# Layer 0 of a hybrid transformer kernel: another order of its first steps, and an end that works by halves of 512 columns

## The chip, the core and the metric

The kernel runs on one core of a Trainium2 chip, as one launch. The core has five engines with queues of their own: TensorE (PE, matrix products), VectorE (DVE), ScalarE (ACT), GpSimd (POOL) and SyncE (SP, which here only issues transfers). They meet at semaphores alone. The metric is the device time of the launch in microseconds.

## The reference

Two layers over 256 tokens of 1024 features, in float32. Each layer normalizes, projects to 13 groups of columns (`w_in`), runs four mixers on them (mLSTM, latent attention with rotary positions, gated linear attention, a convolution), normalizes by group and projects back (`w_out`). Layer 0 then has a dense SwiGLU, layer 1 a mixture of 8 experts of which each token uses two. A last normalization ends it.

```python
h = x
for l in range(DEPTH):                       # DEPTH = 2
    z = rms_norm(h, norm1_g[l]) @ w_in[l]
    (m_qk, m_v, m_o, m_if, a_cq, a_ckv, a_kr,
     g_q, g_k, g_v, g_r, g_a, c_glu) = split_cols(z, IN_SPLITS)
    y = jnp.concatenate([mlstm_mixer(...), mla_mixer(...), gla_mixer(...), conformer_conv(...)], axis=-1)
    h = h + group_rms_norm(y, fuse_g[l], N_GROUPS) @ w_out[l]
    u = rms_norm(h, norm2_g[l])
    f = swiglu(u, ...) if l % 2 == 0 else moe_ffn(u, ...)
    h = h + f
return rms_norm(h, final_norm_g)
```

## The kernel before, in words

Tokens lie on the 128 partitions in two tiles (t = 0, 1); `h[:, t, :]` holds 1024 features. Weights come in pieces of up to 2048 columns, 1 MB each, through a ring of 11 slots that SP fills; a slot is filled again when the piece in it has been split. A piece is split into `high` (ScalarE, line 725) and `low` (VectorE line 1141, for some pieces GpSimd line 622), in three buffers each. TensorE adds three products for each pair of factors (high times high, high times low, low times high); `piece_used` counts the pieces that it is done with and lets ScalarE split the piece three further on.

Every engine's order is written out by hand. In layer 0 the first pieces of `w_in` are `l0` (5 of the 8 blocks of features, 376 columns), `l1` (the other 3 blocks), `b`, `a`, `mq`, `mk` (256 columns, all 8 blocks). `half(name, 0)` and `half(name, 1)` are the two halves of a piece's products. For `l0` and `l1` the half is the token tile; tile 0 lands in bank 2 of PSUM and tile 1 in bank 1, and ScalarE copies them to `zl` (lines 869, 871). `b` lands in bank 0, `a` in bank 5.

Ahead of them TensorE transposes the normalized tokens, two blocks at a time (group g = 0 to 3 of tile t), into the banks of `START_BANKS[0][t][g]`; ScalarE and VectorE empty each bank to `uTh` and `uTl` (lines 759, 1158; `utl_ready` counts the emptied ones). `claim(b, sem, value)` makes TensorE wait until the former owner of bank b has let it go, and notes who lets it go next. Nine small products on bank 0 (line 1836) stand between the transposes and `l0`.

GpSimd first makes constants, issues 12 small loads and computes the angles of the rotary positions (`ang_ready`, line 606), then issues the loads of `walpha`, `uq` and `ukv`, then subtracts for `a`, `mq`, `mk`. ScalarE takes the sine of the angles between its splits of `b` and `a` (line 859, which needs another table of functions than `Ln` and `Exp`). The sines are used by GpSimd in the rotary step (line 662 on), once ScalarE has written the queries out (`q_out`).

At the end, the last expert's products of its hidden values with its last `down` piece fill banks 2 and 3. ScalarE writes both halves of the result as `yh`, VectorE the rest as `yl`; TensorE scatters them to the tokens (`scatter`, four banks); VectorE adds each half to `h` (`add_result`); ScalarE takes the squares of a whole tile, `Ln` and `Exp` for `rstd` (`norm`, `tile_rstd`); VectorE scales a whole tile and SP stores it.

## Time and profile before

| | |
|---|---|
| median of 3 runs | 1259.56 us (1256.64 to 1260.17) |
| the profiled execution's own time | 1260.54 us |
| its span in the trace | 1258.7 us |
| mean granted TensorE clock in it | 0.992 |
| TensorE busy | 98% of the span |
| VectorE, ScalarE, GpSimd busy | 77%, 67%, 14% |
| read from memory | 345.68 MB, 275 GB/s over the span |

The profile cuts the span in 40 slices of 31.5 us. TensorE's busy share is 9 tenths or more in all but the first and the last, which have 6. From about 440 us on, the eight experts follow each other, with memory at about 350 GB/s. Times in the trace are in microseconds from the start of the span; 1.84 us of the execution lie around the span.

### The profile page before, as it was taken

Reading aid. Unit: us, or ns where it says so; the run is one execution under the profiler, and the core shown is the slowest. Engines: PE = TensorE matmul, PEld = TensorE weight load, DVE = VectorE, ACT = ScalarE, POOL = GpSimd, SP = SyncE. Lnnn points to the kernel's source line nnn. Section 1 sums busy time; section 2 is a strip of 40 time slices with the busy share of each in tenths; the row PEclk is TensorE's granted clock in tenths of the full one; section 3 lists DMA queues with packets and bytes.
Section 4 is the critical chain, followed back from the end, with each engine's and each line's share of the span. In section 5 each row is a group of like instructions: output and inputs, shape, how many; then the busy total and the mean of one; then the engine's idle time right before and its main releaser. Section 6 shows DMA issues by size and latency. Waiting matters only on the chain.

```text
span 1258.7 us, 17374 instructions
## 1 busy us (share of the span) xinstructions
PE 1231.3 (98%) x6046; PEld 1026.4 (82%) x6046; DVE 963.1 (77%) x936; ACT 838.9 (67%) x883; POOL 177.4 (14%) x211
## 2 busy tenths in 40 slices
PE   6999999999999999999999999999999999999996
PEld 5888888888888878888888888888888888888885
DVE  4764654545485469999899889989989989988986
ACT  6667643344766767677776677777767767767774
POOL 8765100000486420000000000000000000000000
PEclk9999999999999999999999999999999999999998
DMA  9432975525243399999999999999999999999941
GB/s 305 142 136 67 348 253 181 187 83 168 77 152 125 104 346 353 353 347 364 358 340 361 358 346 353 356 357 352 357 350 349 353 349 358 352 356 347 370 176 52
DMA packets 168912, 347.40 MB, mean 276 GB/s; under 512 B 13166, under 2 KB 44032, under 8 KB 168864
## 3 DMA queue, kind: packets, MB, share of 16 engines
q1 hardware_dynamic: 167600, 344.43, 77.5%
q0 software_dynamic: 1232, 2.33, 0.8%
q8 instruction: 29, 0.48, 0.1%
q14 instruction: 19, 0.16, 0.0%
q10 hardware_dynamic: 32, 0.01, 0.0%
HBM read 345.68 MB, written 1.05 MB: 275 GB/s over the span
## 4 chain that ended last, share of the span: by engine, by line
PE 94%; DVE 3%; POOL 2%; ACT 1%; issue 1%; DVEq 0%; POOLq 0%; ACTq 0%
PE bank L1732 16%; PE bank L1734 16%; PE bank L1733 16%; PE bank L1752 8%; PE bank L1750 8%; PE bank L1751 8%; PE bank L1761 2%; PE bank L1697 2%; PE bank L1699 1%; PE bank L1698 1%; PE bank L1859 1%; PE bank L1860 1%; PE bank L1861 1%; DVE low L1141 1%; PE bank L2198 1%; PE bank L1924 1%
## 5 line engine op out<-in xcount | busy, mean ns | idle before, releaser
L1141 DVE TENSOR_TENSOR low<-ring,high 128x2048 fp32r<-128x2048 f32 (+1 forms) x302 | 684.4, 2286 | 108.9 <-ACT high L725 105.6
L725 ACT ACTIVATE high<-ring 128x2048 fp32r<-128x2048 f32 (+1 forms) x327 | 624.6, 1914 | 189.7 <-PE bank L1734 133.6
L1732 PE MATMUL bank<-high,uTh 128*128 128x512 f32 x880 | 349.7, 397 | 1.0 <-DVE low L1141 0.8
L1734 PE MATMUL bank<-high,uTl 128*128 128x512 f32 x880 | 343.7, 391 | 0.0
L1733 PE MATMUL bank<-low,uTh 128*128 128x512 f32 x880 | 343.5, 390 | 0.0
L1732 PEld LDWEIGHTS bank<-high,uTh 128*128 128x128 f32 x880 | 165.4, 188 | 40.3 <-DVE low L1141 6.3
L1734 PEld LDWEIGHTS bank<-high,uTl 128*128 128x128 f32 x880 | 165.3, 188 | 35.4
L1733 PEld LDWEIGHTS bank<-low,uTh 128*128 128x128 f32 x880 | 165.6, 188 | 32.2
L1750 PE MATMUL bank<-high,moe_hTh 128*128 128x512 f32 x352 | 137.9, 392 | 0.0
L1752 PE MATMUL bank<-high,moe_hTl 128*128 128x512 f32 x352 | 137.3, 390 | 0.0
L1751 PE MATMUL bank<-low,moe_hTh 128*128 128x512 f32 x352 | 137.1, 389 | 0.0
L622 POOL TENSOR_TENSOR low<-ring,high 128x512 fp32r<-128x512 f32 (+1 forms) x67 | 83.2, 1272 | 214.3 <-ACT high L725 210.3
L1752 PEld LDWEIGHTS bank<-high,moe_hTl 128*128 128x128 f32 x352 | 66.1, 188 | 13.8
L1751 PEld LDWEIGHTS bank<-low,moe_hTh 128*128 128x128 f32 x352 | 66.2, 188 | 13.4
L1750 PEld LDWEIGHTS bank<-high,moe_hTh 128*128 128x128 f32 x352 | 66.1, 188 | 13.4
L816 ACT ACTIVATE moe_hTh<-bank 128x512 fp32r<-128x512 f32 (+1 forms) x48 | 27.0, 563 | 66.6 <-PE bank L1761 66.6
L808 ACT ACTIVATE moe_sg<-bank 128x512 f32<-128x512 f32 (+1 forms) x48 | 27.0, 563 | 38.3 <-PE bank L1734 38.3
L1697 PE MATMUL bank<-uTh,high 128*128 128x256 f32 x160 | 48.5, 303 | 4.1 <-ACT zl L869 3.4
L1699 PE MATMUL bank<-uTh,low 128*128 128x256 f32 x160 | 47.5, 297 | 0.0
L1698 PE MATMUL bank<-uTl,high 128*128 128x256 f32 x160 | 47.4, 296 | 0.0
L1268 DVE SCALAR_TENSOR_TENSOR cacc<-bank,cols,cacc 128x255 f32<-128x255 f32 (+29 forms) x120 | 45.7, 458 | 0.1
L630 POOL TENSOR_TENSOR low<-ring,high 128x512 fp32r<-128x512 f32 x32 | 40.9, 1312 | 28.3 <-ACT high L725 28.0
(394 smaller groups left out, 1397.4 us busy)
## 6 DMA issues: line engine op xcount, KB each, us to landing
ring<-in_moe_w_up_dram SPq DMA_DIRECT2D x176, 512.0 KB, 5.5
ring<-in_moe_w_gate_dram SPq DMA_DIRECT2D x176, 512.0 KB, 5.4
ring<-in_moe_w_down_dram SPq DMA_DIRECT2D x176, 512.0 KB, 5.5
ring<-in_w_in_dram SPq DMA_DIRECT2D x36, 512.0 KB, 5.7
ring<-in_ffn_w_up_dram SPq DMA_DIRECT2D x22, 512.0 KB, 4.8
ring<-in_ffn_w_gate_dram SPq DMA_DIRECT2D x22, 512.0 KB, 4.6
ring<-in_ffn_w_down_dram SPq DMA_DIRECT2D x22, 512.0 KB, 4.6
ring<-in_w_out_dram SPq DMA_DIRECT2D x16, 512.0 KB, 4.0
```

Source lines behind the costliest of these rows:

```text
L622: last = pool.tensor_tensor(low[:, n % SPLIT, at], slot(n)[:, at], high[:, n % SPLIT, at].bitcast(F32), ALU.subtract)
L725: act.activation(high[:, n % SPLIT, 0:width], slot(n)[:, 0:width], ACT.Copy).then_inc(s["high_ready"], 1)
L1141: dve.tensor_tensor(low[:, n % SPLIT, 0:width], slot(n)[:, 0:width], high[:, n % SPLIT, 0:width].bitcast(F32), ALU.subtract).then_inc(s["l ...
L1697: pe.matmul(dst, ah, bh, start=first, stop=False)
L1698: pe.matmul(dst, ah, bl, start=False, stop=False)
L1699: last = pe.matmul(dst, al, bh, start=False, stop=final)
L1732: pe.matmul(o, ah, bh, start=(kd == 0), stop=False)
L1733: pe.matmul(o, ah, bl, start=False, stop=False)
L1734: last = pe.matmul(o, al, bh, start=False, stop=(kd == KD - 1))
L1750: pe.matmul(o, ah, bh, start=(c == 0 and f == 0), stop=False)
L1751: pe.matmul(o, ah, bl, start=False, stop=False)
L1752: last = pe.matmul(o, al, bh, start=False, stop=(c == LAST and f == 1))
```

## The change

It has two parts that share no code. **The start of layer 0.** Tile 0's transposes go to banks 2, 0, 1, 4 in place of 0, 4, 1, 2. TensorE takes both tiles of `l0` before `l1`. The nine small products wait for bank 0 but no longer make the `zl` copy its owner, so that `b` need not wait for it. ScalarE takes the sine later, behind the sigmoid of `b`, and the three mask copies ahead of the split of `a`. **The end.** The last `down` piece of each expert is multiplied half by half of its columns (`down_by_half`), and `yh`, `yl`, the scatter, the adds, the squares, the scaling and the stores go by halves of 512 columns, in the order of `LAST_ORDER`. One quarter of the output is scaled in another way: VectorE multiplies by the gain first, ScalarE by `rstd` after it, and ScalarE issues its store.

```diff
+        LAST_ORDER = ((0, 0), (1, 0), (0, 1), (1, 1))
-        START_BANKS = (((0, 4, 1, 2), (3, 5, 7, 6)), ((0, 1, 4, 7), (3, 4, 7, 0)))
+        START_BANKS = (((2, 0, 1, 4), (3, 5, 7, 6)), ((0, 1, 4, 7), (3, 4, 7, 0)))
+        scaled = moe_sg[:, 0, :]
...
-            for t in range(TT):
-                sp.wait_ge(s["out_ready"], t + 1)
-                sp.dma_start(out[0, t * P:(t + 1) * P, :], h[:, t, :]).then_inc(s["stored"], 16)
-            sp.wait_ge(s["stored"], 16 * TT)
+            sp.wait_ge(s["out_ready"], 2)
+            sp.dma_start(out[0, 0:P, :], h[:, 0, :]).then_inc(s["stored"], 16)
+            sp.wait_ge(s["out_ready"], 3)
+            sp.dma_start(out[0, P:2 * P, 512:D], h[:, 1, 512:D]).then_inc(s["stored"], 16)
...
                 split_in("b")
-                if l == 0:
+                if l:
+                    split_in("a")
+                else:
                     act.wait_ge(s["consts"], 1)
-                    act.wait_ge(s["ang_ready"], 1)
-                    act.activation(cossin[:, :, :, :], ang[:, :, :, :], ACT.Sin).then_inc(s["sin_ready"], 1)
-                    act.preload_act_table_set(LN_EXP)
-                split_in("a")
                 for out_, in_ in ((ident_r, ident), (mask_kr, mask_kt), (mask_qr, mask_qt)):
                     last = act.activation(out_[:, :], in_[:, :], ACT.Copy)
                 last.then_inc(s["masks_ready"], 1)
                 if l == 0:
-                    act.wait_ge(s["cols_ready"], 2)
+                    split_in("a")
...
                 act.activation(gsig[:, :, :], tiles2("b", 256), ACT.Sigmoid).then_inc(s["gsig_ready"], 1)
+                if l == 0:
+                    act.wait_ge(s["ang_ready"], 1)
+                    act.activation(cossin[:, :, :, :], ang[:, :, :, :], ACT.Sin).then_inc(s["sin_ready"], 1)
                 act.preload_act_table_set(LN_EXP)
...
             def result_high(n):
-                act.wait_ge(s["piece_used"], N_FFN * n + MOE0)
                 for i in range(2):
-                    last = act.activation(yh[:, i * 512:(i + 1) * 512], bank[2 + i][:, :], ACT.Copy, scale=wslot[:, :])
-                last.then_inc(s["yh_ready"], 1)
+                    if i == 0:
+                        act.wait_ge(s["acc_half"], n)
+                    else:
+                        act.wait_ge(s["piece_used"], N_FFN * n + MOE0)
+                    act.activation(yh[:, i * 512:(i + 1) * 512], bank[2 + i][:, :], ACT.Copy,
+                                   scale=wslot[:, :]).then_inc(s["yh_ready"], 1)
...
-            norm(3, u32[:, :, :].rearrange("p (t k) n -> p t (k n)", t=TT))
+            act.preload_act_table_set(LN_EXP)
+            squares = u32[:, :, :].rearrange("p (t k) n -> p t (k n)", t=TT)
+            for i, (t, half) in enumerate(LAST_ORDER):
+                act.wait_ge(s["h_ready"], 4 * 3 + i + 1)
+                at = slice(half * 512, (half + 1) * 512)
+                chain.done(act.activation(squares[:, t, at], h[:, t, at], ACT.Square, accum_out=ss[:, t, half:half + 1]))
+                chain.wait()
+                if half == 0:
+                    chain.done(act.activation(ss[:, t, 0:1], ss[:, t, 0:1], ACT.Copy, scale=1.0 / D, bias=EPS))
+                else:
+                    chain.done(act.activation(lnv[:, t, 0:1], ss[:, t, 1:2], ACT.Ln, bias=ss[:, t, 0:1], scale=1.0 / D))
+                    chain.wait()
+                    act.activation(rstd[:, t, 0:1], lnv[:, t, 0:1], ACT.Exp, scale=-0.5).then_inc(s["rstd_ready"], 1)
+            act.wait_ge(s["rstd_ready"], 10)
+            act.wait_ge(s["scaled_ready"], 1)
+            act.activation(h[:, 1, 0:512], scaled, ACT.Copy, scale=rstd[:, 1, 0:1]).then_inc(s["out_act"], 1)
+            act.wait_ge(s["out_act"], 1)
+            act.dma_start(out[0, P:2 * P, 0:512], h[:, 1, 0:512]).then_inc(s["stored"], 16)
...
-            for t in range(TT):
-                add_result(n_jobs, 2 * t)
-                add_result(n_jobs, 2 * t + 1)
-                dve.wait_ge(s["added"], 4 * n_jobs - (2 - 2 * t))
-                dve.memset(tiny[:, :], 0.0).then_inc(s["h_ready"], 2)
-            dve.wait_ge(s["rstd_ready"], 10)
+            for i, (t, half) in enumerate(LAST_ORDER):
+                dve.wait_ge(s["scat_ready"], 4 * n_jobs - (3 - i))
+                at = slice(half * 512, (half + 1) * 512)
+                dve.tensor_tensor(h[:, t, at], bank[SCATTER_BANKS[2 * t + half]][:, :], h[:, t, at],
+                                  ALU.add).then_inc(s["h_ready"], 1)
             dve.wait_ge(s["final_in"], 16)
-            for t in range(TT):
-                dve.scalar_tensor_tensor(out=h[:, t, :], in0=h[:, t, :], scalar=rstd[:, t, 0:1], in1=fin_g,
+            dve.wait_ge(s["h_ready"], 4 * 3 + 2)
+            dve.tensor_tensor(scaled, h[:, 1, 0:512], fin_g[:, 0:512], ALU.mult).then_inc(s["scaled_ready"], 1)
+            dve.wait_ge(s["h_ready"], 4 * 3 + 4)
+            for t, half in ((0, 0), (0, 1), (1, 1)):
+                at = slice(half * 512, (half + 1) * 512)
+                dve.wait_ge(s["rstd_ready"], 8 + t + 1)
+                dve.scalar_tensor_tensor(out=h[:, t, at], in0=h[:, t, at], scalar=rstd[:, t, 0:1], in1=fin_g[:, at],
                                          op0=ALU.mult, op1=ALU.mult).then_inc(s["out_ready"], 1)
...
+                def down_by_half(c):
+                    n = n0 + FFN_AT[("d0", c)]
+                    pe.wait_ge(s["hTl_ready"], at(c + 1))
+                    pe.wait_ge(s["low_ready"], pieces + (n + 1))
+                    for half in range(2):
+                        for f in range(2):
+                            bh, bl = part(n, f * 1024 + half * 512, f * 1024 + half * 512 + 512)
+                            pe.matmul(bank[accs[0][half]][:, :], hTh[:, f, 0, :], bh, start=False, stop=False)
+                            pe.matmul(bank[accs[0][half]][:, :], hTh[:, f, 0, :], bl, start=False, stop=False)
+                            last = pe.matmul(bank[accs[0][half]][:, :], hTl[:, f, 0, :], bh, start=False, stop=(f == 1))
+                        if half == 0:
+                            last.then_inc(s["acc_half"], 1)
+                    last.then_inc(s["piece_used"], 1)
...
-                    down(LAST, 0)
+                    down_by_half(LAST)
...
-                    claim(0, "zl_ready", 1)
+                    pe.wait_ge(*owner[0])
...
                 half("l0", 0, ("zl_ready", 2 * l + 1))
-                half("l1", 0)
                 if l:
+                    half("l1", 0)
                     start_transposes(l, 1)
                 half("l0", 1, ("zl_ready", 2 * l + 2))
+                if l == 0:
+                    half("l1", 0)
                 half("l1", 1)
...
-            scatter(n_jobs)
+            pe.wait_ge(s["selT_ready"], n_jobs)
+            for t, half in LAST_ORDER:
+                if t == 0:
+                    pe.wait_ge(s["yl_ready"], 2 * n_jobs - (1 - half))
+                o, at = bank[SCATTER_BANKS[2 * t + half]][:, :], slice(half * 512, (half + 1) * 512)
+                pe.matmul(o, selT[:, t, :], yh[:, at], start=True, stop=False)
+                pe.matmul(o, selT[:, t, :], yl[:, at], start=False, stop=True).then_inc(s["scat_ready"], 1)
```

On ScalarE at the start of layer 0, behind the split of `l1` (`high` is the split, `ring` the loaded piece), before and then of the change:

```order
L725 ACTIVATE high<-ring 128x2048 [waits loaded7]
L859 ACT_TABLE_LOAD [waits ang_ready]
L859 ACTIVATE cossin<-ang 128x64 [waits consts]
L860 ACT_TABLE_LOAD
L725 ACTIVATE high<-ring 128x2048 [waits piece_used,loaded0]
L863 ACTIVATE ident_r<-ident 128x128
L863 ACTIVATE mask_kr<-mask_kt 128x128
L863 ACTIVATE mask_qr<-mask_qt 128x128
L869 ACTIVATE zl<-bank 128x376 [waits tile_done,cols_ready]
```

```order
L730 ACTIVATE high<-ring 128x2048 [waits loaded7]
L866 ACTIVATE ident_r<-ident 128x128 [waits consts]
L866 ACTIVATE mask_kr<-mask_kt 128x128
L866 ACTIVATE mask_qr<-mask_qt 128x128
L730 ACTIVATE high<-ring 128x2048 [waits piece_used,loaded0]
L872 ACTIVATE zl<-bank 128x376 [waits tile_done]
```

The sine and its table have left the queue ahead of the `zl` copies, and with them the wait for the angles. They stand behind the sigmoid (here `y<-bank`), ahead of the squares of the latent norms:

```order
L897 ACT_TABLE_LOAD
L900 ACTIVATE y<-bank 128x512 [waits piece_used]
L903 ACT_TABLE_LOAD
L903 ACTIVATE cossin<-ang 128x64 [waits ang_ready]
L904 ACT_TABLE_LOAD
L908 ACTIVATE junk,lss<-zl 128x192 [waits zl_ready]
```

There they add one table load and the sine to what was a load, the sigmoid and a load. On TensorE, where the transposes of the constants' columns (`y` is their staging buffer) end and the products of `b` begin, before and then of the change:

```order
L1941 MATMUL bank<-ident,y 128x128 [waits utl_ready,rows_in]
L1942 MATMUL bank<-ident,y 128x128
L1697 MATMUL bank<-uTh,high 128x256 [waits zl_ready,low_ready]
L1698 MATMUL bank<-uTl,high 128x256
L1699 MATMUL bank<-uTh,low 128x256
```

```order
L1990 MATMUL bank<-ident,y 128x128 [waits utl_ready,rows_in]
L1991 MATMUL bank<-ident,y 128x128
L1729 MATMUL bank<-uTh,high 128x256 [waits utl_ready,low_ready]
L1730 MATMUL bank<-uTl,high 128x256
L1731 MATMUL bank<-uTh,low 128x256
```

The first product of `b` waited for the `zl` copy and now waits only for bank 0's transposes to be emptied. On ScalarE at the very end, from the writing of `yh` on, before and then of the change:

```order
L1102 ACTIVATE yh<-bank,wslot 128x512 [waits piece_used]
L1102 ACTIVATE yh<-bank,wslot 128x512
L749 ACT_TABLE_LOAD
L740 ACTIVATE u,ss<-h 128x1024 [waits h_ready]
L743 ACTIVATE lnv<-ss,epst 128x1 [waits act_chain]
L745 ACTIVATE rstd<-lnv 128x1 [waits act_chain]
```

```order
L1113 ACTIVATE yh<-bank,wslot 128x512 [waits acc_half]
L1112 ISA
L1113 ACTIVATE yh<-bank,wslot 128x512 [waits piece_used]
L1141 ACT_TABLE_LOAD
L1146 ACTIVATE u,ss<-h 128x512 [waits h_ready]
L1149 ACTIVATE ss<-ss 128x1 [waits act_chain]
L1146 ACTIVATE u,ss<-h 128x512 [waits h_ready]
L1149 ACTIVATE ss<-ss 128x1 [waits act_chain]
L1146 ACTIVATE u,ss<-h 128x512 [waits h_ready]
L1151 ACTIVATE lnv<-ss 128x1 [waits act_chain]
L1153 ACTIVATE rstd<-lnv 128x1 [waits act_chain]
```

The first half of `yh` waits for half of the last piece's products only, and the squares begin with half a tile.

## Rows read from the trace of the kernel before

**Rows 1.** Busy time of each engine in a stretch, granted clock, DMA share, GB/s

```profile
640.00:740.00 100.00, 100.00 (x465) 82.72 (x464) 89.56 (x60) 71.52 (x53) 0.00 (x0) 1.00 0.99 353
```

**Rows 2.** TensorE in order of time: start, us, what, idle before and its releaser

```profile
14.64 0.41 PE L1859 MATMUL bank<-high,uTh 128*128 128x376 f32 x1 [1.92 <-issue]
...
17.99 0.44 PE L1859 MATMUL bank<-high,uTh 128*128 128x376 f32 x1 [0.53 <-DVE low L1141]
...
23.77 0.27 PE L1941 MATMUL bank<-ident,y 128*128 128x128 f32 x1
...
27.55 0.36 PE L1697 MATMUL bank<-uTh,high 128*128 128x256 f32 x1 [3.40 <-ACT zl L869]
...
35.40 0.69 PE L1956 MATMUL bank<-gab,walpha 16*128 16x256 f32 x2
...
36.82 0.36 PE L1697 MATMUL bank<-uTh,high 128*128 128x256 f32 x1
...
42.65 1.02 PE L1977 MATMUL bank<-ukv,ckvT 128*128 128x512 f32 x2
44.30 1.13 PE L1977 MATMUL bank<-ukv,ckvT 128*128 128x512 f32 x2 [0.64 <-DVE mrun L1315]
...
57.26 1.03 PE L1911 MATMUL bank<-ident,qtok 128*96 128x128 f32 x8
```

**Rows 3.** Busy time and granted clock, as in the first group, at 28 to 32

```profile
28.00:32.00 4.00, 4.00 (x24) 4.00 (x23) 1.25 (x2) 2.09 (x4) 3.86 (x4) 0.58 0.84 309
```

**Rows 4.** ScalarE in order of time, at the start

```profile
21.67 1.28 ACT L859 ACT_TABLE_LOAD   x1 [4.39 <-POOL ang L606]
22.96 0.26 ACT L859 ACTIVATE cossin<-ang 128x64 f32<-128x64 f32 x1
...
35.57 1.92 ACT L725 ACTIVATE high<-ring 128x2048 fp32r<-128x2048 f32 x1 [2.20 <-PE bank L1699]
...
44.38 0.24 ACT L909 ACTIVATE rin<-zl 128x64 f32<-128x64 f32 x1
```

**Rows 5.** VectorE in order of time, at the start

```profile
13.42 3.19 DVE L1158 SCALAR_TENSOR_TENSOR uTl<-bank,cols,uTh 128x128 fp32r<-128x128 f32 x12
...
17.97 2.29 DVE L1141 TENSOR_TENSOR low<-ring,high 128x2048 fp32r<-128x2048 f32 x1
...
39.03 5.22 DVE L1315 TENSOR_TENSOR_SCAN mrun<-aj 4x256 f32<-4x256 f32 x1
```

**Rows 6.** GpSimd in order of time, at the start

```profile
23.28 0.57 POOL L641 DMA_DIRECT2D ukv<-in_mla_w_ukv_dram  x1
26.53 10.16 POOL L622 TENSOR_TENSOR low<-ring,high 128x512 fp32r<-128x512 f32 x8 [2.68 <-ACT high L725]
...
38.66 5.04 POOL L622 TENSOR_TENSOR low<-ring,high 128x512 fp32r<-128x512 f32 x4
...
53.51 0.46 POOL L667 TENSOR_TENSOR ktok<-rt 128x128 f32<-128x128 f32 x1
```

**Rows 7.** The load of tile `ukv`, from issue to landing

```profile
DMA to landing us min/median/max: 5.8/5.8/5.8
```

**Rows 8.** All engines in order of time, at the end

```profile
1243.85 1.26 ACT L1102 ACTIVATE yh<-bank,wslot 128x512 fp32r<-128x512 f32 x2 [4.98 <-PE bank L1752]
1245.15 1.41 DVE L1579 SCALAR_TENSOR_TENSOR yl<-bank,wslot,yh 128x512 fp32r<-128x512 f32 x2 [3.66 <-ACT yh L1102]
1246.70 0.77 PE L2216 MATMUL bank<-yh,selT 128*128 128x512 f32 x1 [2.89 <-DVE yl L1579]
1249.71 1.06 ACT L740 ACTIVATE u<-h 128x1024 f32<-128x1024 f32 x1 [3.29 <-DVE tiny L1651]
1250.89 0.29 ACT L743 ACTIVATE lnv<-ss,epst 128x1 f32<-128x1 f32 x1
1253.05 2.48 DVE L1656 SCALAR_TENSOR_TENSOR h<-h,rstd,ring 128x1024 f32<-128x1024 f32 x2 [1.88 <-ACT rstd L745]
1254.37 1.53 SPq L527 DMA_DIRECT2D out_dram<-h  x2
```

More of the change, by code:

```diff
@@ L376, in build @@
                 "gath_ready", "xh_ready", "xl_ready", "selT_ready", "yh_ready", "yl_ready",
-                "scat_ready", "added", "out_ready", "stored",
+                "scat_ready", "added", "acc_half", "scaled_ready", "out_act", "out_ready", "stored",
                 "act_chain", "dve_chain", "pool_chain"):
@@ L524, in _ @@
             sp.dma_start(fin_g, bc(final_norm_g.rearrange("(a d) -> a d", a=1), [P, D])).then_inc(s["final_in"], 16)
-            for t in range(TT):
-                sp.wait_ge(s["out_ready"], t + 1)
-                sp.dma_start(out[0, t * P:(t + 1) * P, :], h[:, t, :]).then_inc(s["stored"], 16)
-            sp.wait_ge(s["stored"], 16 * TT)
+            sp.wait_ge(s["out_ready"], 2)
+            sp.dma_start(out[0, 0:P, :], h[:, 0, :]).then_inc(s["stored"], 16)
+            sp.wait_ge(s["out_ready"], 3)
+            sp.dma_start(out[0, P:2 * P, 512:D], h[:, 1, 512:D]).then_inc(s["stored"], 16)
+            sp.wait_ge(s["stored"], 16 * 3)
         @block.gpsimd
@@ L879, in _ @@
                 act.activation(gln[:, :, :], gln[:, :, :], ACT.Ln, bias=1.0).then_inc(s["gates_ln"], 1)
+                if l == 0:
+                    act.wait_ge(s["cols_ready"], 2)
                 act.wait_ge(s["ckv_tr"], l + 1)
@@ L1109, in slots @@
                     if not first:
-                        act.wait_ge(s["yl_ready"], j)
+                        act.wait_ge(s["yl_ready"], 2 * j)
                     act.activation(selT[:, :, :], bank[7][:, 0:2 * P].rearrange("p (t n) -> p t n", t=TT), ACT.Copy)
@@ L1575, in result_low @@
             def result_low(n):
-                dve.wait_ge(s["yh_ready"], n)
                 for i in range(2):
-                    last = dve.scalar_tensor_tensor(out=yl[:, i * 512:(i + 1) * 512], in0=bank[2 + i][:, :], scalar=wslot[:, :],
-                                                    in1=yh[:, i * 512:(i + 1) * 512].bitcast(F32), op0=ALU.mult, op1=ALU.subtract)
-                last.then_inc(s["yl_ready"], 1)
+                    dve.wait_ge(s["yh_ready"], 2 * n - (1 - i))
+                    dve.scalar_tensor_tensor(out=yl[:, i * 512:(i + 1) * 512], in0=bank[2 + i][:, :], scalar=wslot[:, :],
+                                             in1=yh[:, i * 512:(i + 1) * 512].bitcast(F32), op0=ALU.mult,
+                                             op1=ALU.subtract).then_inc(s["yl_ready"], 1)
             def add_result(n, i):
@@ L1932, in _ @@
                 half("l0", 0, ("zl_ready", 2 * l + 1))
-                half("l1", 0)
                 if l:
+                    half("l1", 0)
                     start_transposes(l, 1)
                 half("l0", 1, ("zl_ready", 2 * l + 2))
+                if l == 0:
+                    half("l1", 0)
                 half("l1", 1)
@@ L2212, in scatter @@
                 pe.wait_ge(s["selT_ready"], n)
-                pe.wait_ge(s["yl_ready"], n)
+                pe.wait_ge(s["yl_ready"], 2 * n)
                 for i, b in enumerate(SCATTER_BANKS):
```

## The prediction, made before the changed kernel ran

> **What bounds the kernel now.** I read the page first: TensorE is busy in every slice but the first and the last. Then stretches: through the experts TensorE is busy for all of a stretch of 100 us, although the DMA engines are busy too [rows 1]. The reader is to see there that the long middle belongs to TensorE, so that time is to be had only where TensorE stands still or runs on half its clock. Then TensorE's instructions in order of time at both ends. At the start it stands still 1.92 us before `l0`, 0.53 before `l1`, 3.40 before `b` (until ScalarE's `zl` copy) and 0.64 before the second product with `ukv` (until VectorE's `mrun`) [rows 2]. Right behind the 3.40 us the granted clock of 28 to 32 is 0.58 [rows 3]: the lower of the two levels, 1.2 GHz, for most of it. ScalarE tells why the copy was late: it stood 4.39 us until GpSimd had the angles, for a sine whose use, the rotary step, ends only at 53.97 [rows 4, 6]. At the end, from 1243.85 on, it is a chain of single steps over whole tiles, ScalarE, VectorE, TensorE, VectorE, ScalarE, VectorE, store [rows 8].
>
> **The start, step by step.** TensorE began `l0` at 14.64 [rows 2], just behind the fourth of VectorE's twelve `uTl` steps (13.42 + 4 x 0.27 = 14.5) [rows 5]: bank 2, where `l0` lands, held the last group of tile 0. Now bank 2 holds the first group, emptied earlier, and `l0` waits only for its own low part, which ended as the `uTl` steps began, at 13.4. I take 13.6. A product of 376 columns costs 0.175 (33 of them from 17.99 to 23.77) [rows 2]. With both tiles of `l0` first (30 products) TensorE comes to `l1` at 18.85, when its low part, done before 17.97 [rows 5], is there. For tile 1 the `uTl` steps are ahead (12 steps end at 16.6, TensorE reaches tile 1 at 16.2 and needs one group in 1.05 us, VectorE makes one in 0.53). So 48 products end at 22.0 and not at 23.77: **1.8 us**.
>
> Behind two transposes (0.35) `b` can start at 22.35; its low part is done at 20.3 (17.97 + 2.29) [rows 5]. Before it started at 27.55. Its 48 products and 4 transposes took 7.85 (to 35.40), where the 48 of `a`, at full clock, took 5.83 (36.82 to 42.65) [rows 2]. With 0.4 for the transposes that is 6.2 if no half clock comes, and `b` ends at 28.55. The `zl` copies don't hold it: ScalarE has split `a` by about 20.8 (it waits for `l0`, 18.85, and takes 1.9), copies tile 0, and tile 1 at 22.1 to 22.5.
>
> Then something else is late. The product with `walpha` waits for four loads on GpSimd's queue, behind the angles, which the change leaves where they are; the last is issued at 23.28 and lands 5.8 later, at 29.1 [rows 6, 7]. So TensorE goes on at 29.15 and not at 35.40: **6.25 us** earlier, 0.6 of it given up to this new wait. Behind it, 1.42 to `a` (30.6): its low part comes from GpSimd, which starts at 23.85 (the issue ends then) and takes half of 10.16 [rows 6], so 29.0. `a` ends at 36.4.
>
> The 0.64 us before the second `ukv` product: `mrun` now starts at 32.8. Its 5.22 us for 4x256 elements [rows 5] look like GpSimd's doing: it ended 0.55 after GpSimd's run of four subtractions (38.66 to 43.70) [rows 6]. Now the run for `mq` ends at 34.1, and GpSimd issues loads for some 2 us before it subtracts for `mk`. I take `mrun` as done by 34.7, long before 37.4. If it takes its 5.22 us all the same, 0.6 is lost again. So the start is worth **6.9 us**, 6.25 at least by this step.
>
> Is ScalarE, with the sine now ahead of the latent norms, late next? From the split of `mk` to the copy to `rin` it took 9.05 (35.57 to 44.62) [rows 4]; one load and the sine add 1.28 + 0.26. It starts when `b` is used, at 28.6, and ends at 39.2, some 0.8 after the `ukv` products; its copies of them (1.5) still end before the queries' products at 41.6. So `q_out` moves with TensorE, and the rotary step, which ended at 53.97 [rows 6], ends near 47.1 for a TensorE that comes at 50.4 (57.26 less 6.9) [rows 2]: 3.3 us of cover. The loads of later pieces hang on freed slots, so they move along; the middle is TensorE's [rows 1], and the 6.9 reach the end.
>
> At this place I weighed a rule of the Trainium skill. The rows show a table load of 1.28 (21.67) with the sine starting at 22.96, right behind it [rows 4]. The page ScalarE: Activation LUTs, section What ACT_TABLE_LOAD costs, counts a drain of about 1.38 us on top, 2.66 a switch. By it three loads would make ScalarE some 4 us later, `q_out` 3.2 us, and the cover would be nearly used up. The sum goes by the row.
>
> **The end**, told in the times of before, without the shift. The first half of the last products is done six products before the whole; at 0.215 (465 in 100 us) [rows 1] that is 1.3, so `yh` starts at 1242.5 and not 1243.85. From [rows 8] a half of `yh` costs 0.65 and a half of `yl` 0.7: `yh` 1242.5 to 1243.15 and 1243.85 to 1244.5, `yl` to 1243.9 and to 1245.25. The first scatter follows the last `down` product with 0.2 us between, where there were 2.89. The four adds, on VectorE behind the second `yl`, go from 1245.3 to 1247.9 (0.65 each, from the nearest row, the 0.7 of `yl`). ScalarE's table is loaded by 1245.8; its first square starts at 1246.0. Two whole tiles took 3.34 (1249.71 to 1253.05); halves add two reads of the sum and two small copies, by estimate 0.2 to 0.3 each (the `Ln` of one column is 0.29), so 4.3: the second `rstd` at 1250.3, the first near 1249.2. VectorE multiplies the quarter by the gain before that, then scales tile 0 (1.24) until 1250.45. The first store goes at 1250.55 and not at 1254.37: **3.8 us**. From there to the end of the span it was 4.3 for 1 MB in two stores 1.2 us apart; now the last two quarters go at 1251.0 and 1251.3, so 4.3 stands. In the experts' loop the products are the same in number, and I count nothing.
>
> Between 3.0 and 4.2: 0.8 less if TensorE still scatters at half clock, 0.4 more if the shorter last store lands sooner.
>
> **The sum.** 1260.54 (the profiled execution's own time) less 6.9 less 3.8 is 1249.8. That execution was 0.98 above the median of the runs, so 1248.9 against the median; I say **1249.0**.
>
> **The rivals.**
> - The half clock comes anyway. For it: TensorE still waits about 0.9 before `l0` and 0.6 for the loads. Against it: 3.40 us of idling are gone, and after the 1.92 us at 12.7 the clock stayed full [rows 2]. Price 7.85 less 6.2, 1.65; with the late `mrun` (0.6) and a late landing 2.5 in all: 1250.6 to 1251.5.
> - The start's gain is taken back in the middle, by loads that come no earlier. For it: DMA share 0.99 [rows 1]. Against it: TensorE has no idle time there, and the loads are issued by freed slots. Then only the end counts: 1259.56 less 3.8, 1255.8.
> - The end doesn't do what it says: the stores alone, or more small steps on ScalarE, set it. Against it: 4.3 us of 15 are the stores. Then 1252.7.
> - The tables cost what the page says. In this kernel that is a first square behind a load that ends 1.2 us later, as the table would be ready at 1247.2: 1250.2. The row at 21.67 [rows 4] speaks against it. (That is the rule named above.)
> - Slower: `down_by_half` puts six products in a row on one bank in each of the 8 experts, where three and three alternated. If that costs TensorE more than 10.7 / 8 = 1.3 us an expert, 0.11 for each of the 12 products, it decides. The products of `up` and `gate` run 12 and 24 in a row on a bank inside the stretch of [rows 1] at the same pace. At twice that price the time would be 1270.
>
> **How the numbers follow.** Forecast 0.70 (its own range 1246.5 to 1251), half clock or late `mrun` 0.13, taken back 0.06, end without gain 0.04, tables 0.04, slower 0.03. The runs before spread over 3.5 us. The range from 1246.0 (both upper bounds and a fast median) to 1254.0 leaves out the taken-back case and the slower one. A measurement here tells 0.3%, 3.8 us, from nothing: faster by more 0.92 (all but half of the taken-back case and the slower one), within it 0.05, slower 0.03.
>
> **What would show it.** Right: `b` starts near 22.4 with no wait for `zl`; 1.00 granted clock from 22 to 32; TensorE's wait before `walpha` ends near 29.1 with the landing; `mrun` short; the head transposes near 50.4 without a wait; the experts at the same pace; at the end the first store 10.7 us earlier in the span. Wrong: an idle TensorE before the queries' transposes (ScalarE late), a slow stretch between 20 and 35, or `down` products above 0.23.

## The result, and the profile of the changed kernel

The changed kernel takes 1251.92 us (median of 6 runs, 1249.82 to 1253.17), the kernel before 1259.72 us (6 runs, 1256.64 to 1260.17): a ratio of 0.9940, 95% interval 0.9926 to 0.9955. It is faster by 0.6%, 7.8 us between the medians. The profiled execution took 1249.98 us with a span of 1248.2, 10.56 less than that of before. The forecast was 1249.0 with a range of 1246.0 to 1254.0, so the time lies inside it, 2.9 us above the forecast. It lies outside the narrower range (1246.5 to 1251) that the prediction gave the forecast itself with 0.70, and 0.4 above the rival of the half clock (1250.6 to 1251.5).

TensorE at the start in order of time, as in [rows 2]:

```profile
13.59 0.44 PE L1906 MATMUL bank<-high,uTh 128*128 128x376 f32 x1 [0.97 <-DVE low L1170]
...
21.95 0.27 PE L1990 MATMUL bank<-ident,y 128*128 128x128 f32 x1
22.05 0.27 PE L1991 MATMUL bank<-ident,y 128*128 128x128 f32 x1
22.08 0.37 PE L1729 MATMUL bank<-uTh,high 128*128 128x256 f32 x1
...
25.04 0.27 PE L1997 MATMUL bank<-ident,zl 128*128 128x128 f32 x1
...
29.84 0.67 PE L2005 MATMUL bank<-gab,walpha 16*128 16x256 f32 x2 [1.32 <-issue]
...
37.06 1.88 PE L2026 MATMUL bank<-ukv,ckvT 128*128 128x512 f32 x4
...
50.77 1.03 PE L1958 MATMUL bank<-ident,qtok 128*96 128x128 f32 x8
```

The reader is to see that `l0` starts at 13.59 and no wait is left until `walpha`; `b` (22.08) follows the transposes at once, where 3.40 us of idling stood before it [rows 2]. The head transposes come at 50.77 and not at 57.26: **6.49 us** earlier. ScalarE, in order of time, as in [rows 4]:

```profile
32.39 1.28 ACT L897 ACT_TABLE_LOAD   x1
33.69 0.60 ACT L900 ACTIVATE y<-bank 128x512 f32<-128x512 f32 x1
34.30 1.28 ACT L903 ACT_TABLE_LOAD   x1
35.60 0.26 ACT L903 ACTIVATE cossin<-ang 128x64 f32<-128x64 f32 x1
35.87 1.28 ACT L904 ACT_TABLE_LOAD   x1
37.17 0.36 ACT L908 ACTIVATE junk<-zl 128x192 f32<-128x192 f32 x1
...
39.63 0.24 ACT L917 ACTIVATE rin<-zl 128x64 f32<-128x64 f32 x1
```

VectorE and then GpSimd in order of time, and the load of `ukv`, as in [rows 5 to 7]:

```profile
25.04 3.95 DVE L1328 SCALAR_TENSOR_TENSOR gb<-gb,gln 128x8 f32<-128x8 f32 x1 [2.04 <-ACT gln L882]
...
33.44 1.21 DVE L1344 TENSOR_TENSOR_SCAN mrun<-aj 4x256 f32<-4x256 f32 x1
```

```profile
23.34 0.57 POOL L646 DMA_DIRECT2D ukv<-in_mla_w_ukv_dram  x1
23.93 10.18 POOL L627 TENSOR_TENSOR low<-ring,high 128x512 fp32r<-128x512 f32 x8
...
47.02 0.46 POOL L672 TENSOR_TENSOR ktok<-rt 128x128 f32<-128x128 f32 x1
```

```profile
DMA to landing us min/median/max: 3.3/4.8/6.4
```

The first of the two loads of `ukv`, issued at 23.34, is the one of 6.4 us: it lands at 29.74, just ahead of the `walpha` product at 29.84. The rotary step ends at 47.48, 3.3 us before TensorE wants it.

The stretch of [rows 1], then that of [rows 3], and two more, with the granted clock third from the right:

```profile
640.00:740.00 100.00, 100.00 (x459) 82.47 (x458) 89.21 (x61) 73.55 (x54) 0.00 (x0) 1.00 0.98 353
28.00:32.00 4.00, 2.67 (x21) 2.10 (x20) 1.97 (x4) 2.79 (x4) 3.86 (x4) 1.00 1.03 375
60.00:66.00 6.00, 6.00 (x35) 5.54 (x34) 5.93 (x14) 2.86 (x12) 3.77 (x4) 0.72 0.46 162
374.00:380.00 6.00, 6.00 (x34) 5.20 (x33) 5.96 (x18) 4.23 (x10) 2.42 (x2) 1.00 0.21 87
```

And the kernel before in the last of these stretches:

```profile
374.00:380.00 6.00, 6.00 (x34) 5.63 (x34) 5.96 (x14) 2.86 (x12) 3.68 (x3) 0.72 0.47 159
```

A mean of 0.72 over 6 us is 3.4 us at the lower level of 1.2 GHz, and about 1.7 us lost. I call such a stretch a half-clock spell. The kernel before had three of them in its body (they began at 27.9, 68.9 and 376.1), the changed one has one (62.0). In the rows above TensorE is busy for all of the 6 us around the spells at 376.1 and at 62.0, and nothing in these rows ties them to the change.

The end, all engines in order of time, as in [rows 8]:

```profile
1234.33 0.69 ACT L1113 ACTIVATE yh<-bank,wslot 128x512 fp32r<-128x512 f32 x1 [3.62 <-PE bank L1799]
1235.05 0.75 DVE L1608 SCALAR_TENSOR_TENSOR yl<-bank,wslot,yh 128x512 fp32r<-128x512 f32 x1 [1.73 <-ACT yh L1113]
1235.69 0.69 ACT L1113 ACTIVATE yh<-bank,wslot 128x512 fp32r<-128x512 f32 x1 [0.67 <-PE bank L1799]
...
1237.73 0.49 PE L2299 MATMUL bank<-yh,selT 128*128 128x512 f32 x1 [2.08 <-DVE yl L1608]
...
1238.50 2.48 DVE L1678 TENSOR_TENSOR h<-bank,h 128x512 f32<-128x512 f32 x4 [1.34 <-PE bank L2300]
...
1242.00 0.20 ACT L1153 ACTIVATE rstd<-lnv 128x1 f32<-128x1 f32 x1
...
1242.31 2.08 DVE L1688 SCALAR_TENSOR_TENSOR h<-h,rstd,ring 128x512 f32<-128x512 f32 x3 [0.72 <-ACT rstd L1153]
...
1243.74 0.35 SPq L529 DMA_DIRECT2D out_dram<-h  x1
```

The last `down` product starts at 1235.26, in the kernel before at 1243.43. I measure the end from there to the end of the span: 12.94 us against 15.27. So the end gave **2.33 us**, not 3.8. The row to look at is the scatter at 1237.73: the first `yl` was there at 1235.80, and TensorE stood still for 2.08. The trace puts the wait down to that `yl`, which had long been done. What TensorE did instead is seen on its queue (`PEldq`, the queue of instructions that feeds it; `ACTq` and `DVEq` are those of ScalarE and VectorE). Here are the rows of the line `with eng.If(n_over > 0)` in `jobs`, which jumps over the loop of overflow jobs when there are none, first of the changed kernel (line 428), then of the kernel before (line 425). The three numbers are the shortest, median and longest duration in ns, the two behind them the first and last start:

```profile
L428 ACTq COMPARE_BRANCH  x1: 50/50/50, 1231.1 to 1231.1; - x1
L428 DVEq COMPARE_BRANCH  x1: 63/63/63, 1231.8 to 1231.8; - x1
L428 PEldq COMPARE_BRANCH  x1: 4023/4023/4023, 1233.5 to 1233.5; - x1
```

```profile
L425 PEldq COMPARE_BRANCH  x1: 3928/3928/3928, 1241.6 to 1241.6; - x1
```

The branch takes ScalarE and VectorE some 50 ns and TensorE's queue 4.0 us. In the changed kernel it ends at 1237.48, 0.25 before the scatter. In the kernel before it ended at 1245.5, before `yl` was done (1246.56), and cost nothing.

### The profile page after: what moved, and what is told of

Its sections match the earlier page's. It is cut to its first block, busy times and chain, and to the rows that moved or that the text cites. A ratio compares the mean times of both kernels' runs of the same rounds, so it can differ in the third digit from the quotient of the medians.

```text
span 1248.2 us, 17388 instructions
## 1 busy us (share of the span) xinstructions
PE 1226.1 (98%) x6046; PEld 1021.6 (82%) x6046; DVE 962.9 (77%) x936; ACT 839.5 (67%) x889; POOL 178.0 (14%) x211
## 3 DMA queue, kind: packets, MB, share of 16 engines
q0 software_dynamic: 1232, 2.33, 0.8%
## 4 chain that ended last, share of the span: by engine, by line
PE 96%; DVE 2%; ACT 1%; DMA 1%; issue 0%; SPq 0%; DVEq 0%; ACTq 0%
PE bank L1764 16%; PE bank L1766 16%; PE bank L1765 16%; PE bank L1784 7%; PE bank L1782 7%; PE bank L1783 7%; PE bank L1808 2%; PE bank L1729 2%; PE bank L1906 2%; PE bank L1730 2%; PE bank L1731 2%; PE bank L1907 2%; PE bank L1908 1%; PE bank L2247 1%; PE bank L1971 1%; PE bank L1973 1%
## 5 line engine op out<-in xcount | busy, mean ns | idle before, releaser
L1782 PE MATMUL bank<-high,moe_hTh 128*128 128x512 f32 x320 | 125.3, 392 | 0.0
L1784 PE MATMUL bank<-high,moe_hTl 128*128 128x512 f32 x320 | 124.7, 390 | 0.0
L1783 PE MATMUL bank<-low,moe_hTh 128*128 128x512 f32 x320 | 124.5, 389 | 0.0
L1784 PEld LDWEIGHTS bank<-high,moe_hTl 128*128 128x128 f32 x320 | 60.1, 188 | 12.7
L1783 PEld LDWEIGHTS bank<-low,moe_hTh 128*128 128x128 f32 x320 | 60.1, 188 | 12.2
L1782 PEld LDWEIGHTS bank<-high,moe_hTh 128*128 128x128 f32 x320 | 60.1, 188 | 12.1
```

Source lines behind the costliest of these rows:

```text
L1782: pe.matmul(o, ah, bh, start=(c == 0 and f == 0), stop=False)
L1783: pe.matmul(o, ah, bl, start=False, stop=False)
L1784: last = pe.matmul(o, al, bh, start=False, stop=(c == LAST and f == 1))
```

## The experiments

They are told in the order of the questions. "Body" is all but the last 20 us; "the end" is the stretch from the start of the last `down` product to the end of the span.

| kernel | profiled, us | half-clock spells in the body | `walpha` product at | the end, us |
|---|---|---|---|---|
| before | 1260.54 | 27.9, 68.9, 376.1 | 35.40 | 15.27 |
| changed | 1249.98 | 62.0 | 29.84 | 12.94 |
| start alone | 1254.56 | 62.5, 369.7 | 29.86 | 16.07 |
| end alone | 1257.99 | 15.1, 28.8, 69.7, 376.9 | 35.84 | 12.54 |
| no branch | 1248.02 | none | 30.53 | 11.57 |
| loads early | 1250.13 | 61.3, 368.5 | 28.59 | 12.92 |
| both of these | 1249.04 | 61.9, 369.1 | 28.52 | 11.54 |
| sine back | 1252.21 | 29.6 | 33.19 | 13.22 |
| owner line back | 1249.32 | none | 30.35 | 13.16 |
| down whole, no branch | 1251.16 | 32.8 | 31.23 | 12.46 |
| branch over a small body | 1250.45 | 31.7, 369.6 | 30.12 | 11.53 |
| changed, again | 1253.26 | 30.8, 64.9, 372.1 | 30.07 | 12.76 |

**The two parts, each alone.** The start's lines of the diff on the kernel before, then the end's lines alone:

```diff
-        START_BANKS = (((0, 4, 1, 2), (3, 5, 7, 6)), ((0, 1, 4, 7), (3, 4, 7, 0)))
+        START_BANKS = (((2, 0, 1, 4), (3, 5, 7, 6)), ((0, 1, 4, 7), (3, 4, 7, 0)))
...
```

> The start's part of the change alone, the end as before. The changed kernel's trace puts the head transposes 6.5 us earlier (57.26 to 50.77) and its first last-half result 8.2 us earlier (1243.85 to 1235.69), 1.7 more, where before had a half-clock spell at 376 and the changed one none. Theory: the start is worth 6.5 whatever the end does, and the rest is spells that come and go with the execution; then this kernel's end keeps before's 14.85 us from the last product to the end of the span, its time is 6.5 below before's (about 1253.2), and executions differ by 1.7 for each spell. Rival: the start's order changes the spells for good; then some 8 us below before in all executions.

```diff
-                    down(LAST, 0)
+                    down_by_half(LAST)
...
-            scatter(n_jobs)
+            pe.wait_ge(s["selT_ready"], n_jobs)
...
```

> The end's part alone, the start as before. Theory: the end is worth what the changed trace shows, 14.85 less 12.51 = 2.3 us, and nothing in the experts' loop: 1257.4. Rival, by the prediction: 3.8 us, if the new start of the changed kernel had disturbed its end. Rival the other way: the down products by half cost something in each of the eight experts; then less than 2.3 in the runs with the end itself still 2.3 shorter in the trace.

The start alone: 1254.56 us against 1259.38 of before, ratio 0.9953 (0.9940 to 0.9967). The end alone: 1257.86, ratio 0.9986 (0.9977 to 0.9995). The parts, 0.47% and 0.14%, add up to the 0.60% of both. For the end alone the interval is 0.6 to 2.9 us, so the run times can't say more exactly what it is worth. With the start alone the `walpha` product waits as in the changed kernel, so that wait comes from the start's part. With the end's part alone the end takes 12.54, 2.73 less than before. In the start alone the branch took 5.51 us, so that the scatter waited for it even with the end as before: the scatter began 0.3 behind the branch's end, after 3.71 of idling where it had 2.89 [rows 8], and that end is 0.80 longer. Scatter in the start alone, the branch ahead of it:

```profile
L425 PEldq COMPARE_BRANCH  x1: 5513/5513/5513, 1234.9 to 1234.9; - x1
```

```profile
1240.72 0.77 PE L2221 MATMUL bank<-yh,selT 128*128 128x512 f32 x1 [3.71 <-DVE yl L1582]
```

**Is it the branch?** The last expert's round was put into the loop of the overflow jobs, so that this loop runs at least once and no branch jumps over it:

```diff
-            with eng.Fori(1, E) as j:
+            with eng.Fori(1, E - 1) as j:
                 body(j, False)
...
-            with eng.If(n_over > 0):
-                with eng.Fori(E, n_over + E) as j:
-                    body(j, False)
+            with eng.Fori(E - 1, n_over + E) as j:
+                body(j, False)
```

> The changed kernel, with the compare and branch around the overflow jobs taken out: the loop over experts 1 to 6 is followed by one over expert 7 and the overflow jobs, so the count is read one expert earlier and no branch stands between the last down products and the scatter. Theory: in the changed kernel TensorE's queue was held by that branch (4.02 us, 1233.46 to 1237.48), so the first scatter came 1.9 us after the first half of yl was there (1235.80 to 1237.73); without it the scatter starts within 0.3 us of the later of the first yl half and the last down product, and the end is 1.3 to 1.5 us shorter: 11.1 us from the second half of yh to the end of the span instead of 12.5. Rival: the wait was for the second half of yl (1237.16); then the scatter still starts after it and nothing is gained.

It took 1250.33 us (5 runs, 1248.02 to 1252.36), ratio 0.9932 (0.9919 to 0.9946), and no branch on TensorE's queue takes over 0.3 us. Its end in order of time, TensorE and VectorE:

```profile
1235.33 0.50 PE L2298 MATMUL bank<-yh,selT 128*128 128x512 f32 x1 [0.21 <-DVE yl L1607]
...
1236.55 2.47 DVE L1677 TENSOR_TENSOR h<-bank,h 128x512 f32<-128x512 f32 x4
```

The scatter now follows with 0.21 us, as the prediction had it, and the adds follow the second `yl` at once. The end is 11.57, 3.70 less than before: the term of 3.8, nearly to the tenth, once the branch is gone. The branch costs the changed kernel 1.37, by the traces; the run times of the two kernels don't tell them apart (their intervals overlap).

**Is it the branch as such, or what it jumps over?** On top of the last kernel, a branch of the same kind, not taken into its body either, but over one wait:

```diff
+            with pe.If(n_jobs > E):
+                pe.wait_ge(s["selT_ready"], E)
             pe.wait_ge(s["selT_ready"], n_jobs)
```

> The kernel without the large branch, with a small one put in its place on TensorE's queue alone: a compare and branch over one wait, on the same count of jobs, which is not taken either way of the computation. Theory: the 4 us are paid for jumping over some 470 instructions of the overflow expert, since ScalarE's and VectorE's branches over about 100 took 0.05 and 0.06 us in the same place; then the small branch takes less than 0.5 us and the scatter starts as early as without any (0.2 us behind the first half of yl). Rival: on TensorE's queue any branch there waits for the products ahead of it to end or costs 3.6 to 5.5 us; then the scatter is 2 us late again.

One execution, 1250.45 us; the scatter is again 0.21 behind `yl`, the end 11.53, and no branch on TensorE's queue takes over 0.3 us:

```profile
1237.76 0.50 PE L2300 MATMUL bank<-yh,selT 128*128 128x512 f32 x1 [0.21 <-DVE yl L1607]
```

So a small branch on the loaded count costs TensorE nothing there; jumping forward over the body of a whole job does. This run leaves something open: it reads the count one expert earlier, where the changed kernel reads it right ahead of the branch. Against that as the cause, ScalarE and VectorE also read it right ahead of theirs, and took 50 and 63 ns. The length of the jump isn't enough either: at the end of each round TensorE's queue jumps back over the same body, and the branch takes 0.21 us in the median of the changed kernel, 0.24 at most. The trace gives a hint of what the 4 us hold. Among the transfers it has some on a queue that it calls instruction. First those on q8 during the branch of the changed kernel (1233.5 to 1237.5), then during that of the start alone (1234.9 to 1240.4), which took longest; the columns are packets, MB and share of 16 engines:

```profile
q8 instruction: 1, 0.02, 2.2%
```

```profile
q8 instruction: 2, 0.03, 4.1%
```

In the changed kernel it is one transfer of 16 KB, 1.2 us behind the start of the branch and 1.4 us long. Each of the eight traces with the branch has such a transfer inside it, and the four without this branch have none in their last 20 us. That fits a wait for code that must be fetched; no run placed the code otherwise to show it, so what the 4 us consist of stays open.

**What is halving the `down` product worth?** The kernel without the branch, with the product whole again:

```diff
-                    if i == 0:
-                        act.wait_ge(s["acc_half"], n)
-                    else:
-                        act.wait_ge(s["piece_used"], N_FFN * n + MOE0)
+                    act.wait_ge(s["piece_used"], N_FFN * n + MOE0)
...
-                    down_by_half(LAST)
+                    down(LAST, 0)
```

> The changed kernel without the branch (as in e3), with the last down product as one piece of 1,024 columns again: both halves of the hidden sum wait for the whole product. Theory (halving the product is worth what one half of the reading takes): the first half's copies can no longer start under the second half of the products, so the scatter starts about 1.3 to 1.5 us later against the last yh than in e3, and the stretch from the second yh to the end, which then begins about where the products end, is 12.4 to 12.7 us instead of 11.14 with both halves of the copies behind it; the whole time is 1.3 to 1.5 us above e3's in executions with the same number of half-clock spells. Rival (TensorE runs ahead, and the halves of the product buy nothing once copies and store are halved): within 0.3 us of e3.

1251.30 us (4 runs), ratio 0.9935 (0.9919 to 0.9952). The end in order of time, ScalarE, TensorE and VectorE:

```profile
1237.37 1.26 ACT L1109 ACTIVATE yh<-bank,wslot 128x512 fp32r<-128x512 f32 x2 [4.98 <-PE bank L1780]
...
1238.89 0.50 PE L2295 MATMUL bank<-yh,selT 128*128 128x512 f32 x1 [1.56 <-DVE yl L1604]
...
1239.67 2.48 DVE L1674 TENSOR_TENSOR h<-bank,h 128x512 f32<-128x512 f32 x4 [0.17 <-PE bank L2296]
```

The scatter is 1.35 later (1.95 behind the start of the last product, where it was 0.60), as expected, but the end is only 0.89 longer (12.46), and the expectation for it was missed: its stretch from the second `yh` (about 1238.0) is 11.4 and not 12.4 to 12.7, and 0.89 is neither the theory's 1.3 to 1.5 nor the rival's 0.3. VectorE makes the second `yl` before the adds in both kernels, so TensorE's lead is used up to that point only: the adds begin 1.82 and 2.73 us behind the start of the last product, 0.91 apart. The halves are worth 0.9 without the branch. In the changed kernel the branch ends 2.2 behind the start of the last product and a whole product lets the scatter go after 1.95, so there they buy next to nothing; that is worked out, not run.

**The wait before `walpha`.** Its loads were put ahead of the angles on GpSimd's queue:

```diff
+            def latent_loads(l):
+                pool.wait_ge(s["norm_tr"], steps_before(3 * l + 1))
+                pool.dma_start(walpha[:, :], gla_w_alpha[l]).then_inc(s["ukv_in"], 16)
...
+            latent_loads(0)
...
+                if l:
+                    latent_loads(l)
```

> The changed kernel, with the four loads of walpha, uq and ukv issued on GpSimd's queue ahead of the angles in layer 0 instead of behind them. Theory: they were late next, TensorE stood 1.32 us before the product with walpha until they had landed (29.7); now they land by about 21, TensorE goes on at 28.5, and all behind it is 1.3 us earlier (head transposes at 49.4). The angles come some 2 us later, 24, and are used at 35. Rival: the low half of a (GpSimd, ended at 29.0) or ScalarE's sine and latent norms take over as what is late, and less than 0.5 us is gained; or the loads push the pieces of w_in behind them, and TensorE waits for a piece instead.

1248.76 us (5 runs, 1246.56 to 1250.13), ratio 0.9910 (0.9896 to 0.9923). TensorE in order of time:

```profile
28.59 0.69 PE L2010 MATMUL bank<-gab,walpha 16*128 16x256 f32 x2
...
35.84 1.88 PE L2031 MATMUL bank<-ukv,ckvT 128*128 128x512 f32 x4
```

The wait is gone, and `ukv` follows 1.22 earlier than in the changed kernel. The rival had a part: the next pieces of `w_in` did come later (ScalarE stood 2.00 us for the load of `a`, and its first `zl` copy began at 21.88, not 20.94), but TensorE didn't wait for it. Then both repairs in one kernel:

> The changed kernel with both of the waits taken away that the prediction had not seen: the four loads ahead of the angles, and no branch ahead of the scatter. Theory: the two gains stand at different ends and add: 1.2 of the loads and 1.4 of the branch, so 2.6 below the changed kernel in executions with equally many half-clock spells; with one spell in the body 1247.3, and 1.7 more for each further one: a median of 1247 to 1249.5. By the step list of the trace: walpha product at 28.6, 11.1 us from the second half of yh to the end of the span. Rival: they overlap in the spells, and the median is that of the early loads alone, 1248.8, or higher.

1248.83 us (5 runs, 1248.02 to 1249.59), ratio 0.9915 (0.9901 to 0.9928). The trace has both gains (`walpha` at 28.52, the end 11.54), yet the median is that of the early loads alone; it lies in the range that was expected and fits the rival as well. The two kernels were run at different times, the kernel before taking 1260.09 us beside this one and 1259.38 beside the other, so the ratios are what to compare, and their intervals overlap. The runs of the early loads include two of 1246.56 and 1246.83 us with a mean granted clock of 0.998; none of this kernel's was above 0.997. Less two spells of 1.7 each, the two profiled executions would be 1246.7 and 1245.6. That the branch's removal is worth its 1.4 here too is so argued from the trace; the medians don't show it.

**Which line of the start does it?** The sine back at its old place, the rest as changed:

```diff
+                    act.wait_ge(s["ang_ready"], 1)
+                    act.activation(cossin[:, :, :, :], ang[:, :, :, :], ACT.Sin).then_inc(s["sin_ready"], 1)
+                    act.preload_act_table_set(LN_EXP)
+                split_in("a")
...
```

> The changed kernel with ScalarE's queue as before (the sine ahead of the split of a, the masks behind it); TensorE's order, the banks and the owner of bank 0 as changed. Theory: TensorE starts b at 22.4 all the same, since it no longer waits for the zl copy, but stands right behind it: the transposes of zl need the copies, which ScalarE makes only at about 27 (sine and tables until 24.5, split of a until 26.4). So TensorE idles from 25.2 to about 27.5, b's second half ends near 30.6 and not 28.5, and the product with walpha, which waited for the loads until 29.8 in the changed kernel, comes at about 30.7: only 0.9 us of the 6.5 are lost, since the late loads hide the rest. Rival: all of the 3.4 us come back, and the product with walpha is at 33 or later.

One execution, 1252.21 us; TensorE in order of time:

```profile
28.26 0.30 PE L1994 MATMUL bank<-ident,zl 128*128 128x128 f32 x1 [3.11 <-ACT zl L876]
...
33.19 0.69 PE L2002 MATMUL bank<-gab,walpha 16*128 16x256 f32 x2
...
54.15 1.03 PE L1955 MATMUL bank<-ident,qtok 128*96 128x128 f32 x8
```

I had expected `walpha` at 30.7 and was wrong; by the number the rival, all comes back, was right. But not all of it is the wait: the `zl` transposes came 0.8 later than I took (28.26), and from them to the `walpha` product it took 4.93 us where the kernel with early loads took 3.40, which is the half-clock spell. The wait for the late `zl` copy only moves from the front of `b` to its middle, where the `zl` transposes stand, and the spell follows at 29.6. The head transposes are 3.38 later than in the changed kernel. And the line that keeps `zl` from owning bank 0 undone alone:

```diff
-                    pe.wait_ge(*owner[0])
+                    claim(0, "zl_ready", 1)
```

> The changed kernel with bank 0 owned by the zl copy again (b waits for it); the sine stays late. Theory: the zl copy of tile 0 is done at 21.4, before the transposes of the constants' columns end at 22.3, so this line alone is worth nothing here: b at 22.4, the product with walpha at 29.8, as in the changed kernel. Rival: b starts later by the copy's end and sync, by 0.5 us or more.

One execution, 1249.32 us: the `zl` transposes come at 25.05, where they came at 25.04; `walpha` is 0.5 later for its loads, which land at 30.26. With the copies early that line is worth nothing. In the run before, with the copies late, it let `b` start (22.04), but the wait came back in the middle of `b`; the move of the sine is what takes it away.

**The changed kernel once more.**

> The changed kernel once more, unchanged. Theory (the spread between its executions is the number of stretches of 3.4 us in which TensorE is granted half its clock inside the body, 1.7 us each): the profiled execution is 1250.0 if it shows one such stretch before the end's, and 1251.7 with two, 1253.4 with three, and the start and the end take the same as in the first profile within 0.7 us (walpha's product by 29.2 to 30.5, the end from the second yh 12.2 to 12.9). Rival (the spread has another source): the time differs from the first profile's by over 0.7 us with the same number of stretches.

1253.13 us (4 runs, 1252.73 to 1255.68), ratio 0.9954 (0.9937 to 0.9970); the profiled execution 1253.26 with three spells. The stretches after the `walpha` product, granted clock third from the right:

```profile
28.00:32.00 4.00, 2.68 (x16) 1.94 (x15) 1.72 (x2) 2.59 (x3) 3.86 (x4) 0.85 1.03 373
32.00:36.00 4.00, 4.00 (x28) 3.97 (x26) 3.41 (x7) 3.91 (x6) 4.00 (x5) 0.73 0.61 181
```

Two spells more than in the first profile and 3.28 us more, 1.64 each: the theory held. Start (30.07) and end (12.76) are within 0.25 of the first profile. With as many spells as the kernel before, the changed kernel gains 7.28, not 10.56.

## Why the prediction was right, and where it was off

**What held.** `l0` began at 13.59 (forecast 13.6), the 48 products ended at 21.95 (22.0), `b` started at 22.08 without a wait (22.35) and its products ran at full clock. A new wait came before `walpha` and ended with the landing of `ukv`. `mrun` took 1.21 and not 5.22 us, and the second `ukv` product no longer waited. The rotary step's cover was 3.3 us as forecast. The experts' pace is the same. These are TensorE's steps of the loop over the experts in the kernel before and in the changed one, with the times of the first and the last of seven:

```profile
L421 PEldq ALU_OP  x7: 32/32/32, 652.7 to 1240.5; - x7
```

```profile
L424 PEldq ALU_OP  x7: 32/32/32, 644.7 to 1232.3; - x7
```

Six experts take 587.8 and 587.6 us, where the slower rival, six `down` products in a row on a bank, wanted at least 1.3 an expert, 7.8 in all; it fell. No gain was taken back in the middle: 6.5 at the head transposes is 8.2 at the end of this loop, the spell at 376.1 making the rest.

**Table loads.** Behind each of the three the next activation began 1.30 us after the load's start (32.39 to 33.69, 34.30 to 35.60, 35.87 to 37.17). At the end the first square (1239.23) waited for `h`, not for the table. The Trainium skill, page ScalarE: Activation LUTs, section What ACT_TABLE_LOAD costs, counts a drain of 1.38 on top: these rows don't show one, and the sum by the row was right.

**The start: 6.9 was 6.5.** The step "the last is issued at 23.28 and lands 5.8 later, at 29.1" took the landing of another execution: 6.4 us here, 29.74. So the `walpha` product came at 29.84, and the step gave 5.56 in place of 6.25; the second `ukv` product gave back 0.9 in place of 0.64. The rival of the half clock is half true: 1.65 of the 6.25 counted on no half clock behind `b`'s start. All three traces with a late `zl` copy (before, end alone, sine back) have a spell at 27.9 to 29.6. Of the seven whose TensorE waits for `walpha`'s loads instead, three have one at 30.8 to 32.8; the two with early loads, where it waits for nothing, have none. The start is worth 6.5 without it and 4.7 with it (head transposes at 52.58 in the second profile). A spell costs nothing where a later wait takes it up: the one at 15.1 in the end alone fell ahead of the wait for the `zl` copy, and `b` started 12.91 us behind `l0` there, as in the kernel before.

**The end: 3.8 was 2.3**, below its own bounds of 3.0 to 4.2. The step that failed is "The first scatter follows the last `down` product with 0.2 us between, where there were 2.89". I read the idle row as a wait for `yl` alone, and beneath it lay a second one, the branch, which ended 1.2 us before that scatter and was hidden. With it gone the step and the term hold (0.21, and 3.70).

**The sum.** 6.5 and 2.3 are 8.8; a spell at 376 that the profiled execution didn't have added 1.7, which is why 10.56 looks like the forecast's 10.7: that is luck, and so is the first store, 10.6 us earlier (1254.37 to 1243.74). The medians differ by 7.8. The forecast was 2.9 below the median for three reasons: 1.5 at the end, 0.4 at the start, and the profiled execution's distance to the median (0.98), which was taken off the sum. This last step had no ground, since that distance changes with the spells of the one execution that was profiled. 1260.54 less 6.5 and 2.3 is 1251.7, 0.2 from the measured median. The range held because it had room for the rivals, not because the end was right.

## What to carry to other kernels

Before you count a stall as removed, look at the queue of the waiting engine for branches, loop ends and register loads that lie under the wait: they become the wait when the semaphore comes early. When a step is taken out of an engine's queue, count every later use of what it delayed; a wait that is only let through at one place comes back at the next. Changes worth some 2 us in 1250 need the half-clock spells counted in each trace before two times are compared. The best kernels here are those with the early loads, 1248.8 us with or without the branch.

## What the runs showed of the hardware

A forward jump over the body of one job took TensorE's queue 3.6 to 5.5 us in eight executions, and 50 and 63 ns on the queues of ScalarE and VectorE. One round of that body has 450 products and 449 weight loads recorded on TensorE, 59 busy instructions on VectorE and 53 on ScalarE. In each of the eight, at least one transfer of 16 KB on an instruction queue falls into the branch.

On VectorE an operation of 8 columns took 3.95 us while GpSimd did its eight subtractions of 512 columns, and the scan `mrun` took 5.22 beside four of them [rows 5, 6], 1.21 where they ended 0.67 after its start, and 0.68 in the changed kernel's second profile, where they had ended. That looks like GpSimd stretching VectorE's small operations. But to stand beside them isn't enough: in the kernel before the same operation of 8 columns took 0.17 (at 30.19), with the same eight subtractions running since 26.53. No run took the subtractions away, so the cause stays open. In the changed kernel neither held TensorE up.
